# Conditioning sums of the first stage: from VectorE to GpSimd, with one load of the memory instead of two

## The reference

```python
def hybrid_mixer(x, mem, w_in, ...):
    proj = x @ w_in                       # 28 column blocks of 128: xa, ba, ca, u, v, xc, da, dg, q, gate
    y_a = short_gated_conv(xa, ba, ca, conv_a_w)
    y_b = spatial_gating(u, v, sg_ln_g, sg_ln_b, sg_w, sg_b)      # layer norm of gelu(v), then a mix over tokens
    y_c = multiscale_pool(xc, pool_w, pool_scale)
    y_d = conformer_conv(da, dg, ...)                             # a depthwise convolution of 31 taps
    y_e = memory_cross_attention(q, mem, w_kv)                    # k and v are mem @ w_kv
    h = jnp.concatenate([y_a, y_b, y_c, y_d, y_e], axis=-1) * jax.nn.silu(gate)
    return h @ w_out
...
cond = jax.nn.silu(c)                                             # 1024 numbers
mod = (cond @ ada_w[layer] + ada_b[layer])                        # ada_w: 2 x 1024 x 6144
shift1, scale1, gate1, shift2, scale2, gate2 = jnp.split(mod, 6, axis=-1)
hn = rmsnorm(x, norm1_w[layer]) * (1 + scale1) + shift1
```

## Time and profile before

| | |
|---|---|
| median of 3 runs | 2209.98 us (2206.01 to 2212.12) |
| the profiled execution | 2209.98 us, span of the trace 2208.3 us |
| mean granted clock of TensorE | 0.97 of full speed |
| busy share: TensorE, VectorE, ScalarE, GpSimd | 97%, 33%, 23%, 12% |
| first stage | 0 to 247 us of the span |
| `stage_out` with its norm | 247 to about 381 us |

### The profile page before, as it was taken

How to read it: one execution, slowest core, us unless ns; L and a number is a source line. 1 busy time by engine, 2 the same in 40 slices (tenths; PEclk the granted TensorE clock), 3 DMA queues, 4 the chain that set the end, 5 groups by cost and what they waited for, 6 DMA issues and landing times. The chain is left out here.

```text
span 2208.3 us, 24933 instructions
## 1 busy us (share of the span) xinstructions
PE 2149.9 (97%) x9870; PEld 1446.4 (65%) x9870; DVE 719.2 (33%) x998; ACT 517.0 (23%) x884; POOL 273.4 (12%) x291
## 2 busy tenths in 40 slices
PE   8999998999999999999999999999999999999997
PEld 5444456666544444446445666675599999999996
DVE  2675233345652333310002466766210000000013
ACT  1321003433421000000004657753212111111111
POOL 2000112000001111100001444443120000000011
PEclk9999986999999999997999999999999999999998
DMA  9323630111113555522211211110295676678883
GB/s 339 102 63 114 232 104 10 58 57 48 49 39 123 191 191 190 193 70 105 70 56 57 68 48 49 57 48 10 82 312 196 192 249 236 226 277 307 301 326 138
DMA packets 81374, 308.18 MB, mean 140 GB/s; under 512 B 9849, under 2 KB 10369, under 8 KB 81137
## 3 DMA queue, kind: packets, MB, share of 16 engines
q1 hardware_dynamic: 60912, 238.05, 31.9%
q0 software_dynamic: 14496, 51.48, 6.7%
q10 hardware_dynamic: 5856, 17.13, 2.2%
HBM read 297.30 MB, written 9.33 MB: 139 GB/s over the span
## 5 line engine op out<-in xcount | busy, mean ns | idle before, releaser
L243 PE MATMUL banks<-sb_x_norm,sb_ring 128*128 128x512 f32 x1344 | 592.7, 600 | 3.9 <-ACT sb_x_norm L400 3.9
L2099 PE MATMUL banks<-sb_act,sb_ring 128*128 128x192 f32 (+3 forms) x3696 | 500.9, 298 | 1.5 <-ACT sb_act L2153 0.8
L2099 PEld LDWEIGHTS banks<-sb_act,sb_ring 128*128 128x128 f32 x3696 | 498.3, 191 | 2.6 <-DMA sb_ring<-in_w_moe_up 1.2
L243 PEld LDWEIGHTS banks<-sb_x_norm,sb_ring 128*128 128x128 f32 x1344 | 255.7, 193 | 314.5 <-issue 311.7
L2378 DVE TENSOR_TENSOR sb_act<-sb_work,banks 128x128 f32<-128x128 f32 (+3 forms) x88 | 27.7, 315 | 514.4 <-PE banks L2099 514.3
L243 PE MATMUL banks<-sb_x_res,sb_ring 128*128 128x512 f32 x448 | 194.4, 593 | 0.0
L243 PE MATMUL banks<-sb_act,sb_ring 128*128 128x512 f32 x352 | 153.8, 600 | 3.1 <-PEq L1374 3.1
L243 PEld LDWEIGHTS banks<-sb_x_res,sb_ring 128*128 128x128 f32 x448 | 84.7, 190 | 104.9 <-issue 104.9
L243 PEld LDWEIGHTS banks<-sb_act,sb_ring 128*128 128x128 f32 x352 | 67.8, 193 | 88.3 <-issue 88.3
L254 PEld LDWEIGHTS banks<-sb_ring,sb_x_norm 128*128 128x128 f32 x1024 | 117.6, 194 | 2.5 <-issue 2.4
L254 PE MATMUL banks<-sb_ring,sb_x_norm 128*128 128x128 f32 x1024 | 118.7, 278 | 0.0
(11 more groups left out here) (365 smaller groups left out, 1944.4 us busy)
## 6 DMA issues: line engine op xcount, KB each, us to landing
sb_ring<-in_w_moe_up SPq DMA_DIRECT2D x176, 512.0 KB, 4.6
sb_ring<-in_w_moe_down SPq DMA_DIRECT2D x64, 704.0 KB, 5.9
sb_work<-in_cond_w POOLq DMA_DIRECT2D x44, 512.0 KB, 4.6
sb_ring<-in_w_ffn_up SPq DMA_DIRECT2D x44, 512.0 KB, 4.1
sb_ring<-in_w_h_in SPq DMA_DIRECT2D x32, 512.0 KB, 3.5
sb_ring<-in_w_in SPq DMA_DIRECT2D x28, 512.0 KB, 3.7
sb_act<-in_cond_w POOLq DMA_DIRECT2D x28, 512.0 KB, 4.8
sb_ring<-in_w_m_in SPq DMA_DIRECT2D x24, 512.0 KB, 3.6
```

The lines of the kernel that those rows point to most:

```text
L243: last = m.nc.tensor.matmul(bank[:, 0:act.shape[2]], w[:, rows(k, P)], act[:, k, :], start=(k == 0), stop=(k == kt - 1))
L2099: last = nc.tensor.matmul(ps[:, b % BANKS, 0:cap], w, act, start=(k == 0), stop=(k == kt - 1))
```

## The change

The weighing of the groups 0 to 2 moves from VectorE to GpSimd. There it is two instructions for each chunk (a multiplication by the scalar in place, and an addition to the sum), in one program with the loads, which now go through 4 buffers. There are 2 buffers for sums, so group 2 begins when TensorE has read the sum of group 0. TensorE does the sums over the partitions within the first stage: groups 0 and 1 behind `norm_v.mean`, group 2 behind `pool_groups`, each waiting for GpSimd. VectorE finishes the three groups at the end of the first stage, and only groups 3 and 4 in `stage_out`. The memory is loaded in one piece ahead of the first weights. Counts of semaphores in `stage_out` and `stage_ffn` follow; nothing else changes there.

```diff
-    chunk = [wide(m.HN[:, 6:8, :]), wide(W[:, 14:16, :]), wide(W[:, 16:18, :])]
-    sums = m.first_sums = [wide(m.HN[:, 2 * c:2 * c + 2, :]) for c in range(FIRST_GROUPS)]
+    chunk = [wide(m.HN[:, 4:6, :]), wide(m.HN[:, 6:8, :]), wide(W[:, 14:16, :]), wide(W[:, 16:18, :])]
+    sums = [wide(m.HN[:, 0:2, :]), wide(m.HN[:, 2:4, :])]
...
-            sp.dma_start(m.memT[:, 0:KD // 2, :], a["memT"][:, 0:KD // 2, :]).then_inc(m.s_mem, 16)
-            load_first(m, sp, kv, 1)
-            sp.dma_start(m.memT[:, KD // 2:, :], a["memT"][:, KD // 2:, :]).then_inc(m.s_mem_rest, 16)
-            load_first(m, sp, kv, 4, 1)
+            sp.dma_start(m.memT, a["memT"]).then_inc(m.s_mem, 16)
+            load_first(m, sp, kv)
...
             pool.wait_ge(m.s_x, 16)
             load(0)
+            load(1)
...
             pool.wait_ge(m.blocks_done, kv.done + kv.n)
-            load(1)
             load(2)
-            for n in range(FIRST_CHUNKS, FIRST_GROUPS * KD):
-                pool.wait_ge(m.chunk_used, n - FIRST_CHUNKS + 1)
-                load(n)
+            load(3)
+            pool.wait_ge(m.s_cond, 1)
+            for c in range(FIRST_GROUPS):
+                if c >= 2:
+                    pool.wait_ge(acc_done, c - 1)
+                for k in range(KD):
+                    n = c * KD + k
+                    pool.wait_ge(chunk_in[n % CHUNKS], 16 * (n // CHUNKS + 1))
+                    src, total, w = chunk[n % CHUNKS], sums[c % 2], m.cond[:, k:k + 1]
+                    if k == 0:
+                        step(nc.gpsimd.tensor_scalar(total, src, w, None, ALU.mult))
+                    else:
+                        step(nc.gpsimd.tensor_scalar(src, src, w, None, ALU.mult))
+                        step(nc.gpsimd.tensor_tensor(total, total, src, ALU.add))
+                    if n + CHUNKS < FIRST_GROUPS * KD:
+                        load(n + CHUNKS)
+                pool.sem_inc(acc_ready, 1)
...
+            def spread_sums(c):
+                pe.wait_ge(acc_ready, c + 1)
+                spread_group(m, sums[c % 2], 7, c).then_inc(acc_done, 1)
...
             norm_v.mean(m, pe)
+            spread_sums(0)
+            spread_sums(1)
             project(XA + 1)
...
             pool_groups()
+            spread_sums(2)
             project(GATES[1])
...
-            dve.wait_ge(m.s_cond, 1)
-            conditioning(0, 12)
+            dve.wait_ge(m.s_par, 16)
             ready(DGT + 1)
...
-            for i, name in enumerate(GATES):
+            for name in GATES:
                 ready(name)
                 tile = W[:, name - GATE, :]
                 step(nc.vector.tensor_tensor(tile, tile, A[:, name, :], ALU.mult))
-                if i < 6:
-                    conditioning(12 + 2 * i, 14 + 2 * i)
+            dve.wait_ge(acc_done, FIRST_GROUPS)
+            finish_conditioning(m, step, 0, FIRST_GROUPS, ps[:, 7, 0:8 * FIRST_GROUPS], ((0, 0, "norm1"),))
...
                 if b == KD - 2:
-                    for c in range(EARLY_GROUPS):
-                        if c >= FIRST_GROUPS:
-                            pe.wait_ge(m.acc_ready, c - FIRST_GROUPS + 1)
-                        spread_group(m, (m.first_sums + sums)[c], 7, c).then_inc(m.acc_done, 1)
+                    for c in range(FIRST_GROUPS, EARLY_GROUPS):
+                        pe.wait_ge(m.acc_ready, c + 1)
+                        spread_group(m, sums[c - FIRST_GROUPS], 7, c).then_inc(m.acc_done, 1)
```

More of the change, by code:

```diff
@@ L177, in c, with load_first @@
         return self.cst[:, a:b]
-def load_first(m, sp, plan, last=SLOTS, first=0):
+def load_first(m, sp, plan):
     w = plan.kt * P
-    for s in range(first, min(last, plan.n)):
+    for s in range(min(SLOTS, plan.n)):
         if plan.free[s]:
@@ L423 @@
 N_SMALL, N_LATER = 12 * 16, 4 * 16
-GROUPS, FIRST_GROUPS, EARLY_GROUPS, FIRST_CHUNKS = 12 * D // COND, 3, 5, 3
+GROUPS, FIRST_GROUPS, EARLY_GROUPS = 12 * D // COND, 3, 5
 def weigh(m, step, src, out, k):
@@ L476, in stage_first @@
     m.memT = W[:, 14:18, :].rearrange("p a (b c) -> p (a b) c", c=MEM)
-    m.s_mem, m.s_mem_rest, m.s_x, m.s_par, m.s_small, m.s_cond = (m.sem(n) for n in (
-        "mem_loaded", "mem_rest_loaded", "x_loaded", "par_loaded", "small_loaded", "cond_ready"))
+    m.s_mem, m.s_x, m.s_par, m.s_small, m.s_cond = (m.sem(n) for n in (
+        "mem_loaded", "x_loaded", "par_loaded", "small_loaded", "cond_ready"))
     chunk_in = m.chunk_in = [m.sem(f"cond_loaded{i}") for i in range(CHUNKS)]
     m.chunk_used, m.acc_ready, m.acc_done = (m.sem("cond_" + n) for n in ("used", "summed", "out"))
+    acc_ready, acc_done = m.acc_ready, m.acc_done
     (vn_ready, vt_ready, vt_out, mixed, mixed_used, conv_done, conv_ready, conv_act, pw_done,
@@ L509, in load @@
             def load(n):
-                pool.dma_start(chunk[n % FIRST_CHUNKS], m.cond_w[n]).then_inc(chunk_in[n % FIRST_CHUNKS], 16)
+                pool.dma_start(chunk[n % CHUNKS], m.cond_w[n]).then_inc(chunk_in[n % CHUNKS], 16)
             pool.wait_ge(m.s_x, 16)
             load(0)
+            load(1)
             pool.wait_ge(m.s_small, N_SMALL)
@@ L660, in _ @@
             nc.scalar.activation(m.cond[:], m.p("c"), ACT.Silu).then_inc(m.s_cond, 1)
-            act.wait_ge(m.s_mem_rest, 16)
+            act.wait_ge(m.s_mem, 16)
             for out, src in ((m.gw[:], a["gw"]), (m.sgw[:], a["sgw"]), (m.plw[0:64, 0, 0:64], a["plw"][0]),
@@ L748, in _ @@
             ready = lambda name: dve.wait_ge(m.evac, out_of(name))
[L750 to L754, removed]
             def taps(first, last):
@@ L958, in _ @@
                     dve.wait_ge(m.acc_done, EARLY_GROUPS)
-                    finish_conditioning(m, step, 0, EARLY_GROUPS, ps[:, 7, 0:8 * EARLY_GROUPS],
-                                        ((0, 0, "norm1"), (0, 1, "norm2")))
+                    finish_conditioning(m, step, FIRST_GROUPS, EARLY_GROUPS,
+                                        ps[:, 7, 8 * FIRST_GROUPS:8 * EARLY_GROUPS], ((0, 1, "norm2"),))
             dve.wait_ge(mean, 1)
@@ L979, in _ @@
                 if n >= CHUNKS:
-                    act.wait_ge(m.chunk_used, begun + n - CHUNKS + 1)
+                    act.wait_ge(m.chunk_used, n - CHUNKS + 1)
                 act.dma_start(chunk[n % CHUNKS], m.cond_w[begun + n]).then_inc(chunk_in[n % CHUNKS], 16)
@@ L1372, in stage_ffn @@
     pairs = SLOTS // 2
-    earlier = [len(range(i, FIRST_GROUPS * KD, FIRST_CHUNKS)) if i < FIRST_CHUNKS else 0 for i in range(CHUNKS)]
     with nc.Block() as block:
@@ L1382, in _ @@
             product(m, pe, plan, by_features(m, m.HN, KD), first=by_features(m, m.HN, KD, norm.need(m, pe)))
-            pe.wait_ge(m.acc_ready, GROUPS - FIRST_GROUPS)
+            pe.wait_ge(m.acc_ready, GROUPS)
             for c in range(late):
@@ L1391, in _ @@
                 if n >= CHUNKS:
-                    pool.wait_ge(m.chunk_used, EARLY_GROUPS * KD + n - CHUNKS + 1)
+                    pool.wait_ge(m.chunk_used, (EARLY_GROUPS - FIRST_GROUPS) * KD + n - CHUNKS + 1)
                 pool.dma_start(chunk[n % CHUNKS], m.cond_w[EARLY_GROUPS * KD + n]).then_inc(chunk_in[n % CHUNKS], 16)
@@ L1425, in conditioning @@
                 c, k = divmod(n, KD)
-                dve.wait_ge(chunk_in[n % CHUNKS], 16 * (earlier[n % CHUNKS] + n // CHUNKS + 1))
+                dve.wait_ge(chunk_in[n % CHUNKS], 16 * ((FIRST_GROUPS * KD + n) // CHUNKS + 1))
                 weigh(m, step, chunk[n % CHUNKS], sums[c], k)
```

5 lines of the change are left out of this document (1 added, 4 removed).

## The result

The changed kernel takes 2220.24 us (median of 6 runs, 2217.79 to 2221.32), the kernel before 2206.90 (6 runs): the ratio is 1.0056, 95% interval 1.0045 to 1.0067. It is 13 us slower.

The account below looks back on a forecast made before the run. TensorE, busy for 97% of the span, was taken as the bound. Its 58.3 us delay at `turn_values`, +1.3 +1.9 +1.9 -10.3 +0.6 +1.3 +1.3, gave 56.3 on 2209.98: 2266 us, range 2220 to 2292 (the forecast's own 2246 to 2288).

Parts of the forecast that it names:

- where the slacks are: VectorE in the first stage is early by 4.1 us at `softmax(0)`, 4.6 at `softmax(1)`, 4.6 at the normed `v`.
- The sums in `stage_out`: Five groups' sums over partitions take 14.1 us there; with two groups at the fast rate 3.8, saving 10.3.
- Clock and sums behind `turn_values`: First stage: 1.9 us for TensorE's clock behind the third stall, 1.9 for the sums of group 2.
- The step that failed: A GpSimd multiplication was taken to hold VectorE's taps like an addition; bounds were holding nothing and 3.12 us.
- The ledger: First-stage tally of chunks on GpSimd against VectorE's work, making TensorE 58.3 us late at `turn_values`.
- 7.0 us in which three taps get through: A GpSimd chunk beside VectorE's taps takes 7.0 us, and three taps pass in it instead of nine.
- first stall: TensorE waits 6.9 us ahead of the third block after the first scores, as `softmax(0)` is held up.
- the second: TensorE stalls about 20 us ahead of `turn_probs(1)`, because `softmax(1)` ends late.
- the third: TensorE stalls some 24 us ahead of `turn_values`, because the normed `v` is late.
- Rival A: GpSimd's multiplication is short, or doesn't hold VectorE: 2216 to 2232 us, chance 0.18.
- The configuration of the multiplication: GpSimd's first multiplication brings a configuration costing between nothing and 4.0 us while VectorE is idle; +1.3 counted.
- The head: With the whole memory loaded ahead of the first weights, the first matmul starts at about 9.4 instead of 8.1: +1.3 us.

Follow-up runs that it names:

- a_no_weigh: The changed kernel with GpSimd weighing only the first chunk of each group (3 multiplications, no additions): 2205.32 us, 0.9988 of the kernel before.

## Why the prediction was wrong

**What held.** What bounds the kernel and where the slacks are; that VectorE's 34 us of weighing gain nothing (in `a_no_weigh` VectorE is rid of it and GpSimd too, but for three multiplications, and `turn_values` is still 7.0 later than before). GpSimd's lengths: 2.94 and 2.34 estimated, 2.86 and 2.34 measured. The addition holds VectorE nearly for its whole length. The sums in `stage_out`: 10.3 less estimated, 10.6 measured (3.5 for 14.1); from out's first block to the first gate matmul it is 10.2 shorter. Clock and sums behind `turn_values`: 3.8 estimated, 3.5 measured (24.9 less 21.4). The waits at `turn_probs(1)` and `turn_values` are there and come from VectorE.

**The step that failed** is the one that had no row: "For the multiplication the trace shows no such meeting; I take it to hold like the addition, the nearest row." The ledger lets it hold VectorE for 2.6 us; a tap that meets it loses 1.3 of its 2.86. With it fell "7.0 us in which three taps get through": it is 6.4 with four, so VectorE loses 3.3 us to a chunk and not 4.7. This is mis-sized by nearly a third, but the ledger turns it into stalls only beyond slacks of 4 to 5 us, and there the error grows: the taps ahead of `softmax(0)` end at 71.4 instead of 77.4, `softmax(0)` is done at 82.7 instead of 91.4, so the first stall (6.9) does not happen; the second is 8.1 instead of 20, the third 2.6 instead of 24. From the end of the centring to the normed `v` VectorE needs 27.2 us (143.9 to 171.1), 11.0 more than before, where the ledger had 26.2 more. At `turn_values` TensorE is 21.4 late and not 58.3.

**Rival A** named this case (0.18) and gave 2216 to 2232, 6 to 22 us more than before; with 13 more the result lies there. I had set against it only the length of a multiplication. Its length was right, and its hold was another thing. Rival A is half right itself: the multiplication is not short, and it does hold VectorE, for a part. Its upper edge rested on GpSimd being late with group 1, and that did not happen: the group was done at 123.7, its sum over the partitions began at 140.7. So the agreement in number is partly luck, and it is luck too that 2220.24 lies within 2220 to 2292. The Trainium skill's rule (SBUF — State Buffer, Who interferes with whom), that whoever starts first keeps the shared port for its whole instruction, fits the additions here (a tap ends 0.54 behind one) and not the multiplications: a tap of 0.75 passes beside the last 1.2 us of one, and the tap at 86.28, which by the profile began first, was held by the one at 86.63. The measurement decides.

**The small terms.** `finish_conditioning` at the end of the stage: 0.6 said, nothing measured; from the start of the last gate product to out's first block it is 2.46 before and 2.45 after. The configuration of the multiplication: 1.3 said, nothing seen; it begins at 27.93, as soon as the loads are issued. The head: 1.3 said; 2.1 in one profile and 1.1 in the other, of which the load is about 1; unsettled in the whole time. The last block of `stage_out`, left as it was: 1.3 gained.

**The range** rested on the held multiplication too. Its bound "holding nothing" was there, but it went into the rivals and not into the centre.

## What to carry to other kernels

Work moved from VectorE to GpSimd is paid twice: it takes longer there (5.2 us for 1.28 here), and VectorE stands still for a part of it. Count the part held for each kind of instruction from a row in which the two meet, and where there is none, put the centre between the bounds. A long run of single-column matmuls cost time by the clock that was lost in it and behind it: 14.1 us for five groups in one run, with 11.8 for the block behind them, against 5 times 1.84 and 8.8 when they stood one by one between dense blocks.

## What the runs showed of the hardware

A GpSimd multiplication of 1024 fp32 columns takes 2.86 us and delays a two-input VectorE instruction of 0.75 by 1.3 us at most, half the width by 0.7; an addition takes 2.34 and delays it by 2.0, and by 2.5 where additions alone follow each other. Matmuls with one column: 0.115 us each in runs of 16 and 32 (1.84 and 3.63), 0.204 with the clock at its lower level. And one stretch of the same instructions took 331.3 and 338.7 us in two executions of one kernel, at a mean granted clock of 0.98 and 0.96: two profiles should not be subtracted before that is looked at.
